# Relative-position bias images written by eight four-head transfers on ScalarE's queue instead of thirty-two one-head transfers on SyncE's

## The reference, cut to what matters

```python
rel = positions[:, None, :] - p_blk[:, :, None]
bias = rel_table.astype(jnp.float32)[t5_bucket(rel)]
s = s + bias.transpose(0, 3, 1, 2)[:, :, None]
p = jax.nn.softmax(s, axis=-1)
```

## Time and profile before

| | us |
|---|---|
| three runs | 2514.42, 2518.47, 2519.95 |
| median | 2518.47 |
| the profiled execution | 2514.42 |
| its span | 2512.7 |
| TensorE busy | 2284.7 (91%) |
| ScalarE busy | 701.4 (28%) |
| DMA, mean over the span | 105 GB/s |
| granted TensorE clock, mean | 0.945 |

### The profile page before, as it was taken

The page is one execution under the profiler, slowest core; times in us unless marked ns, Lnnn a source line. Parts: engine busy times, 40 slices in busy tenths (PEclk is TensorE's granted clock), DMA queues, the critical chain, the costliest instruction groups (busy, mean ns, idle before and its releaser), DMA issues. The chain is left out here.

```text
span 2512.7 us, 29091 instructions
## 1 busy us (share of the span) xinstructions
PE 2284.7 (91%) x11596; PEld 1867.8 (74%) x11596; DVE 1441.7 (57%) x2138; ACT 701.4 (28%) x862; POOL 746.1 (30%) x439
## 2 busy tenths in 40 slices
PE   5999987997889999999999989889965898999986
PEld 3887875676667888888888878778845686878875
DVE  4665435894648887677765663329881424731223
ACT  4104412675122222222222223224124322111121
POOL 0212220112517656655662221110000541221240
PEclk8999988999989999999999996899978998999998
DMA  6596421333113333333332111252236322111111
GB/s 244 209 304 183 125 93 52 109 111 134 43 42 97 111 104 105 116 113 113 113 119 73 51 42 67 76 160 83 96 98 197 146 114 70 51 42 51 42 51 67
DMA packets 108303, 264.98 MB, mean 105 GB/s; under 512 B 9415, under 2 KB 52839, under 8 KB 105065
## 3 DMA queue, kind: packets, MB, share of 16 engines
q1 hardware_dynamic: 105172, 258.04, 31.1%
q10 hardware_dynamic: 3000, 5.15, 0.6%
HBM read 222.79 MB, written 57.13 MB: 111 GB/s over the span
## 5 line engine op out<-in xcount | busy, mean ns | idle before, releaser
L2342 POOL TENSOR_TENSOR w_lo<-w_staged,w_hi 128x1024 fp32r<-128x1024 f32 x66 | 162.5, 2462 | 371.6 <-ACT w_hi L2437 371.5
L233 POOL TENSOR_TENSOR w_lo<-w_staged,w_hi 128x1024 fp32r<-128x1024 f32 (+1 forms) x34 | 83.2, 2449 | 254.8 <-ACT w_hi L200 254.7
L1263 PE MATMUL ps_in<-h_hi,w_hi 128*128 128x512 f32 x400 | 126.6, 398 | 9.4 <-DVE h_lo L648 9.1
L1255 POOL TENSOR_TENSOR w_lo<-w_staged,w_hi 128x1024 fp32r<-128x1024 f32 x23 | 58.1, 2527 | 229.1 <-ACT w_hi L1242 229.1
L366 POOL TENSOR_TENSOR w_lo<-w_staged,w_hi 128x1024 fp32r<-128x1024 f32 x24 | 58.0, 2418 | 228.4 <-ACT w_hi L349 228.4
L374 PE MATMUL ps_odd<-o_hi,w_hi 128*128 128x512 f32 x384 | 121.0, 397 | 4.2 <-DVE o_lo L648 4.2
L1263 PE MATMUL ps_in<-h_lo,w_hi 128*128 128x512 f32 x400 | 124.4, 392 | 0.0
L1263 PE MATMUL ps_in<-h_hi,w_lo 128*128 128x512 f32 x400 | 124.0, 391 | 0.0
L2437 ACT CAST w_hi<-w_staged 128x1024 fp32r<-128x1024 f32 x66 | 69.0, 1045 | 188.4 <-PE ps_dn L2378 188.4
L2248 DVE SCALAR_TENSOR_TENSOR ada_acc<-x_ctx,cond,ada_acc 128x512 f32<-128x512 f32 x112 | 119.8, 1100 | 2.0
L374 PE MATMUL ps_odd<-o_lo,w_hi 128*128 128x512 f32 x384 | 118.8, 391 | 0.0
(11 more groups left out here) (473 smaller groups left out, 5648.5 us busy)
## 6 DMA issues: line engine op xcount, KB each, us to landing
w_staged<-in_w_ff SPq DMA_DIRECT2D x66, 512.0 KB, 3.6
x_ctx<-in_w_ada SPq DMA_DIRECT2D x48, 512.0 KB, 5.1
x_in<-in_w_ada SPq DMA_DIRECT2D x16, 1024.0 KB, 8.0
scratch_bias<-scratch_line SPq DMA_DIRECT2D x32, 512.0 KB, 7.5
att_bias<-scratch_bias SPq DMA_DIRECT2D x32, 512.0 KB, 3.2
w_staged<-in_w_in SPq DMA_DIRECT2D x17, 512.0 KB, 4.6
ada_w<-in_w_ada SPq DMA_DIRECT2D x8, 1024.0 KB, 19.4
scratch_cp<-ff_shared SPq DMA_DIRECT2D x16, 384.0 KB, 5.8
```

The lines of the kernel that those rows point to most:

```text
L233: nc.gpsimd.tensor_tensor(st.lo[i % 2][:, 0:widths[i]], st.staged[i % 2][:, 0:widths[i]], st.hi[i % 2][:, 0:widths[i]].bitcast(F32), ALU.s ...
L1255: nc.gpsimd.tensor_tensor(st.lo[i % 2][:, :], st.staged[i % 2][:, :], st.hi[i % 2][:, :].bitcast(F32), ALU.subtract).then_inc(st.split, 1)
L1263: last = nc.tensor.matmul(ps[i % 2][:, a:a + BANK], u[i % 2][:, k * P:(k + 1) * P], r[:, k, a:a + BANK], start=(k == 0 and part == 0), sto ...
L2342: nc.gpsimd.tensor_tensor(st.lo[i % 2][:, :], st.staged[i % 2][:, :], st.hi[i % 2][:, :].bitcast(F32), ALU.subtract).then_inc(st.split, 1)
```

## The change

`bias_image` takes a tile of queries for all four heads at once: the source pattern has an outer dimension of 4 (a step of one line), then 128 rows, then 1024 elements. There are 8 such transfers of 2 MB. They are issued from ScalarE's list, one behind each of the casts 12 to 19, and no longer from SyncE's. The semaphore's goal becomes 16 x 8.

```diff
--- before.py
+++ after.py
@@ -1127,7 +1127,6 @@
     ROUNDS = {12: (0, 0), 14: (0, 1), 16: (1, 0), 18: (1, 1)}
     SLOTS_OF = tuple(ROUNDS)
     READY = 2
-    IMAGE = 8
     PIECES = 8
     FIRST = 4
     HALF = KD // 2 * BANK
@@ -1201,9 +1200,6 @@
                 if 0 <= at < N_IN - OWN:
                     sp.wait_ge(placed, at + OWN + 1)
                     sp.dma_start(g.dram["spill"][at], place[at % 2]).then_inc(spilled[at % 2], 16)
-                if IMAGE <= i < IMAGE + TT * HEADS // 2:
-                    for piece_of in range(2 * (i - IMAGE), 2 * (i - IMAGE) + 2):
-                        bias_image(g, sp, image_stored, piece_of)
             for s in range(2):
                 sp.wait_ge(spilled[s], 16 * ((N_IN - OWN) // 2))
 
@@ -1240,6 +1236,8 @@
                 act.wait_ge(st.loaded[i % 2], loads[i % 2] + 16 * (i // 2) + 16)
                 act.wait_ge(st.done, base + i - 1)
                 nc.scalar.copy(st.hi[i % 2][:, :], st.staged[i % 2][:, :]).then_inc(st.hi_ready, 1)
+                if 12 <= i < 12 + TT:
+                    bias_image(g, act, image_stored, i - 12)
                 if i - 1 in ROUNDS:
                     first_half(SLOTS_OF.index(i - 1), *ROUNDS[i - 1])
                 if i - 2 in ROUNDS:
@@ -1688,13 +1686,12 @@
         act.dma_start(self.g.dram["line"], self.line).then_inc(self.stored, 16)
 
 
-def bias_image(g, engine, image_stored, piece):
-
-
-
-    t, h = piece // HEADS, piece % HEADS
-    rows = bass.AP(tensor=g.dram["line"].tensor, offset=h * LINE + L - P - t * P, ap=[[LINE, 1], [1, P], [1, L]])
-    engine.dma_start(g.dram["bias"][h:h + 1, t * P:(t + 1) * P, :], rows).then_inc(image_stored, 16)
+def bias_image(g, engine, image_stored, t):
+
+
+
+    rows = bass.AP(tensor=g.dram["line"].tensor, offset=L - P - t * P, ap=[[LINE, HEADS], [1, P], [1, L]])
+    engine.dma_start(g.dram["bias"][:, t * P:(t + 1) * P, :], rows).then_inc(image_stored, 16)
 
 
 def diff_lambda(nc, g, lam, ctx):
@@ -1793,7 +1790,7 @@
                 sp.dma_start(pos_q[:, :], g.dram["pos_columns"]).then_inc(loaded, 16)
                 sp.dma_start(table[:, :, :].rearrange("p b h -> p (b h)"), g.dram["rel_row"].to_broadcast([P, BUCKETS * HEADS])).then_inc(loaded, 16)
                 sp.dma_start(edges[:, :], g.dram["edges"].to_broadcast([P, EDGES])).then_inc(loaded, 16)
-                sp.wait_ge(image_stored, 16 * TT * HEADS)
+                sp.wait_ge(image_stored, 16 * TT)
                 for t in range(TT):
                     sp.wait_ge(by_dve, (t + 1) * C)
                     sp.dma_start(g.dram["bias"][:, t * P:(t + 1) * P, :].rearrange("h p k -> p h k"), bias[:, :, :]).then_inc(stored, 16)
```

## The result

| | before | after |
|---|---|---|
| median, us | 2517.53 (4 runs, 2514.42 to 2519.95) | 2564.72 (4 runs, 2561.18 to 2565.81) |
| ratio | | 1.0187, 95% [1.0176, 1.0200] |
| the profiled execution, us | 2514.42, span 2512.7 | 2565.6, span 2564.0 |
| granted TensorE clock, mean | 0.945 | 0.939 |

The change costs 47 us. The two profiled spans differ by 51.3 us; 4 of these come from which execution was profiled (the one of before lies 3.1 us under its median, that of after 0.9 above).

The account below looks back on a forecast made before the run. TensorE was taken to bound the input projections. From the profiled 2514.4 us, 0 for SyncE and DMA relief, 0 for ScalarE's issues and +60 for the backlog gave 2574.4; with 4.05 for the median, 2578 us. Range 2563 to 2603, 8-in-10 2514 to 2597.

Parts of the forecast that it names:

- the term that matters: Input projections: image backlog delays unit 21 by 55 us, plus 5 for the clock, +60 us.
- that case: Input projections: held-up weights or casts, +45 to +85 us, 2563 to 2603 us; chance 0.58.
- the headline step: Input projections: SyncE's weight load waits behind an image not yet handed over, so unit 21 starts 55 us late.
- TensorE bounds the stage, and relief of SyncE and of the full stretch is worth 0: Input projections: 32 fewer SyncE issues and 16.8 MB less from 121 to 175 us gain 0, at most 1 us.
- Eight issues more on ScalarE cost 0 as long as they stay short: Behind casts 12 to 19: issues of 0.47 to 1.69 us cost 0, at most 1 us.
- Outer dimension 4 means four engines, 20.5 us an image, done at 372 us: Image transfers from 183 us: four engines, 20.5 to 23.8 us an image against one every 12.3, done at 372 or 400.
- A weight load that SyncE issues behind a waiting image waits too: Load of unit 21, behind the last image: handed over at 352 us, unit 21 starts at 359.5 instead of 304.8.
- My addition to it: Rival, 183 to 372 us: backlog holds up nobody, price 0, 2518 to 2524 us; chance 0.30 together with 16 engines.
- ScalarE itself held, the last image taken at 352, unit 20 at 355.5 instead of 293.0, +62: Rival at cast 20: the image issue itself lasts, 2581 us; counted with the forecast in the 0.58.
- One image held, from the start's 124 rows: Image queue: hardware holds 124 rows of 4 KB an engine, about one 128-row image; the next waits.
- 5 us for the clock behind the last pause: Input projections: TensorE's clock drops while it pauses, adding 5 us after the last paced unit.
- The bound of 82 us, with 186 ns a row and one image held: Unit 21's delay: other sizes beside the 55 us taken were 75 with next to nothing held and 34 with two images.

Follow-up runs that it names:

- the last experiment: Changed kernel with the image issue moved to the end of ScalarE's turn, behind gate activations and value copy; 2554.03 us, ratio 1.0144 against the kernel before.
- half tiles: Changed kernel with each image cut into two transfers of 64 rows and four heads, both behind the same cast, still four engines; 2576.89 us, ratio 1.0231.
- two engines: Changed kernel with each image cut into two transfers of two heads, both issued by ScalarE behind the same cast; 2723.39 us, ratio 1.0813.
- every second cast: Changed kernel with its eight images issued behind casts 8, 10, ... 22 instead of 12 to 19; 2518.69 us, ratio 1.0001.

## Why the prediction was right in the time, and where a step of it was wrong

*The forecast was 2578 us; 2564.7 came.* The sign and the term that matters (one stall, at the end of the backlog) held. The range of that case, 2563 to 2603, held by 2 us, and not on its merits alone: two errors of opposite sign lie in the term, and without the 11 us of gate chain that the forecast left out, the time would have been the 2554.0 of the last experiment, below that range. Which engine would be held, the headline step, was wrong. Point by point:

- **TensorE bounds the stage, and relief of SyncE and of the full stretch is worth 0.** Right: TensorE is full in both kernels up to 200 us, with a DMA share of 0.61 or 1.00.
- **Eight issues more on ScalarE cost 0 as long as they stay short.** The condition failed; under it the statement is right, since 32 short ones cost nothing either.
- **Outer dimension 4 means four engines, 20.5 us an image, done at 372 us.** Right: 4128 packets of 160 ns, the last at 367. That the count of engines alone decides is shown by the image with the same bytes and sixteen engines.
- **A weight load that SyncE issues behind a waiting image waits too.** This step was wrong. The loads landed after 6.4 us in the median instead of 3.9, 2.5 us longer, with some 17 us of room, and the waits from 45 to 480 us (total, times, longest) hold for this stage's casts (line 1238) one that waited for a transfer, the one near 82 us that the earlier trace rows has too:

```profile
ACT w_hi L1238 <- DMA w_staged<-in_w_in: 9.6, 1, 9.6
```

  The 5.8 against 3.4 us of the earlier trace rows was of just this size, a somewhat longer landing, and I read it as a door that shuts for both. What the runs show: the queue that issues the narrow transfers is held, and only it. The issue on ScalarE lasted 16.2 us in the median; with the images on SyncE the loads behind them landed 28.8 us after the start of an issue that itself took 19, and the kernel was at 2574.5. The rule from the Trainium skill that the prediction set against its own step ("Queues, rings and completion order", alternation between queues packet by packet) fits this: SyncE's loads slipped between. My addition to it, that therefore nobody is held up, does not follow: the issuer is.
- **ScalarE itself held, the last image taken at 352, unit 20 at 355.5 instead of 293.0, +62.** This rival, counted with the forecast, is what happened, at +46: unit 20 started at 338.9. Two sizes in it were off and partly cancel. The last image was taken at 323.5 and not 352, since the hardware held 252 rows an engine at that moment and not 128; at 160 ns this is 20 us, and the rest is that the images ran 5 us ahead of the forecast and small differences. Against it, 11 us of gate chain stand between that issue and cast 20, which I left out and the last experiment measured.
- **One image held, from the start's 124 rows.** Mis-sized: it is about 84 rows and a whole transfer on top, and for the last image, which decides, 123 and a whole transfer. The start's figure was bytes over sixteen engines with other sizes of packet; it isn't a constant of the queue.
- **5 us for the clock behind the last pause.** Not found. The clock fell to 0.64 in 250 to 275 us, in the middle of the stalls, and was 1.00 from 325 us on, and the stage's shift of 46.2 us is the delay of unit 20 alone.
- **The bound of 82 us, with 186 ns a row and one image held.** A slip in the sum: 400 - 23.8 + 7.45 - 304.8 is 79. The range does not hang on it.

What stays open: what the 84 rows are made of, in descriptors or bytes, which no run varied apart from the rows; and why some transfers are taken with about 40 rows more left than the others. It is not the end of the series that does it but the count: in every kernel here where ScalarE was held it is the eighth transfer (252 in the kernel after, 192 with half tiles, 255 on two engines, no wait at all with every second cast), and where there are sixteen, the sixteenth too (188, 254).

## What to carry to other kernels

Before a DMA is regrouped into fewer, larger ones, look at its outermost dimension and count its packets: the number of engines may shrink with it, and the same bytes then take longer: the eight images kept each of four engines busy for 165 us (0.219 x 16 x 188 / 4), and each of sixteen for 71 us (0.616 x 115). Compare transfer time with the pace at which transfers are issued; above it, the issuing engine itself stops, and everything behind that issue in its program order pays. If a narrow transfer can't be avoided, space it out, keep it off the queue that prefetches, and issue it behind the work that others wait for, not in front of it.

## What the runs showed of the hardware

- A DMA issue on ScalarE is not always a short instruction: it lasted 0.7 us with little outstanding and up to 21.5 us (25.6 with two engines) with a backlog in its queue, and ScalarE's compute behind it stood.
- On SyncE the held instruction was the one behind the image: an image issue of 1.2 us, then a load issue of 19.4 us.
- What ScalarE's queue had outstanding when an issue ended is not a fixed number of rows: 212 to 215 with 128-row transfers, 148 in the median with 64-row ones, on each of four engines. Every eighth transfer was taken some 40 rows earlier (252; 192 and 188).
- A row of 4 KB takes 0.158 to 0.160 us of one engine where two or four engines share the transfer, 0.152 where eight do, and 0.268 where sixteen do.
- Scratch-to-scratch copies with 2 MB a transfer, on sixteen engines, landed after 16.2 us in the median at a DMA share of 0.91, and TensorE had no gap beside them.
